# Two gelu buffers, sums of squares on VectorE behind the residual, and a side product moved forward in a two-block network

## The reference, cut to what matters

```python
h = rms_norm(x, g_mix_pre)
z = h @ w_in                                   # pool, recurrent, gelu and gate columns
xc = causal_dwconv(u_rx, conv_w, conv_b)       # 4 taps
r, i = sigmoid(xc @ w_gates + b_gates)         # 16 heads of 64, block diagonal
a = exp(-8 r softplus(-lambda)); mult = sqrt(1 - a^2)
h_t = a_t h_{t-1} + mult i xc                  # scan over the tokens
y_rnn = (h * gelu(u_rg)) @ w_rg_out
merged = sigmoid(g1) * y_pool + sigmoid(g2) * y_rnn
x = x + rms_norm(merged @ w_o, g_mix_post)
up = rms_norm(x, g_ffn_pre) @ w_up             # 2 x 3072
x = x + rms_norm((gelu(causal_dwconv(up[:, :3072])) * up[:, 3072:]) @ w_down, g_ffn_post)
gate = sigmoid(rms_norm(x, g_ple_gate) @ w_ple_gate)
x = x + gate * rms_norm(p @ w_ple_proj, g_ple_post)   # p: 1024 x 256
```

## Time and profile before

| | |
|---|---|
| median of 3 runs | 3355.74 us (3354.76 to 3365.66) |
| the profiled execution's own time | 3357.36 us |
| its span, first to last instruction | 3355.5 us |
| PE busy | 3221.1 us (96%) |
| PEld busy | 2582.4 us (77%) |
| DVE, ACT, POOL busy | 1538.5, 748.9, 1122.4 us |
| mean granted clock of PE | 0.994 of 2.4 GHz |
| mean transfer rate over the span | 62 GB/s |

### The profile page before, as it was taken

How to read it: one execution, slowest core, us unless ns; L and a number is a source line. 1 busy time by engine, 2 the same in 40 slices (tenths; PEclk the granted TensorE clock), 3 DMA queues, 4 the chain that set the end, 5 groups by cost and what they waited for, 6 DMA issues and landing times.

```text
span 3355.5 us, 41945 instructions
## 1 busy us (share of the span) xinstructions
PE 3221.1 (96%) x17662; PEld 2582.4 (77%) x17662; DVE 1538.5 (46%) x1625; ACT 748.9 (22%) x961; POOL 1122.4 (33%) x525
## 2 busy tenths in 40 slices
PE   6999998999889999899999999999999999999999
PEld 5877876787668788798576788788788888888757
DVE  3134428328822423824766601442553154255476
ACT  1011225112211122511334501112301011001241
POOL 2232220135532232044133344453144344434323
PEclk9999999999999999999999999999999999999999
DMA  6210111332131011112111111112211111111212
GB/s 235 70 32 14 39 35 48 126 137 84 61 119 38 14 38 47 57 42 109 63 51 38 38 44 54 38 54 97 76 49 45 50 50 44 50 50 45 81 44 75
DMA packets 59243, 208.16 MB, mean 62 GB/s; under 512 B 5856, under 2 KB 7648, under 8 KB 59104
## 3 DMA queue, kind: packets, MB, share of 16 engines
q1 hardware_dynamic: 42240, 143.15, 13.3%
q10 hardware_dynamic: 16864, 62.97, 5.0%
HBM read 188.27 MB, written 17.83 MB: 61 GB/s over the span
## 4 chain that ended last, share of the span: by engine, by line
PE 75%; DVE 16%; ACT 5%; DMA 2%; issue 1%; ACTq 0%; DVEq 0%
PE ps L541 65%; DVE Sb L1748 3%; PE ps L800 2%; DMA modfirst<-modw 1%; DVE stage L1839 1%; PE ps L523 1%; PE ps L568 1%; PE ps L710 1%; PE ps L1037 1%; PE ps L625 1%; DVE xc L1970 1%; DVE Y L1834 1%; DMA xin<-xT 1%; PE ps L947 1%; DVE stage L1854 1%
## 5 line engine op out<-in xcount | busy, mean ns | idle before, releaser
L467 POOL TENSOR_TENSOR w_hi<-raw,pool_zero 128x1024 fp32r<-128x1024 f32 (+2 forms) x242 | 454.0, 1876 | 2139.1 <-PE ps L541 2065.7
L469 POOL TENSOR_TENSOR w_lo<-raw,w_hi 128x1024 fp32r<-128x1024 f32 (+2 forms) x242 | 633.4, 2617 | 19.0
L541 PE MATMUL ps<-h_hi,w_hi 128*128 128x512 f32 (+1 forms) x1832 | 491.0, 364 | 26.5 <-ACT QK L1101 15.4
L541 PE MATMUL ps<-g_hi,w_hi 128*128 128x512 f32 x1568 | 490.5, 394 | 10.2 <-DVE g_lo L1574 5.2
L541 PE MATMUL ps<-g_lo,w_hi 128*128 128x512 f32 x1568 | 483.1, 389 | 0.0
L541 PE MATMUL ps<-g_hi,w_lo 128*128 128x512 f32 x1568 | 482.8, 389 | 0.0
L541 PE MATMUL ps<-h_lo,w_hi 128*128 128x512 f32 (+1 forms) x1832 | 469.7, 352 | 0.0
L541 PE MATMUL ps<-h_hi,w_lo 128*128 128x512 f32 (+1 forms) x1832 | 469.4, 352 | 0.0
L541 PEld LDWEIGHTS ps<-h_hi,w_hi 128*128 128x128 f32 x1832 | 301.0, 189 | 100.2 <-issue 23.3
L541 PEld LDWEIGHTS ps<-g_hi,w_hi 128*128 128x128 f32 x1568 | 292.9, 188 | 82.6 <-issue 9.4
L541 PEld LDWEIGHTS ps<-g_lo,w_hi 128*128 128x128 f32 x1568 | 294.4, 188 | 61.5
(11 more groups left out here) (312 smaller groups left out, 3451.2 us busy)
## 6 DMA issues: line engine op xcount, KB each, us to landing
raw<-s SPq DMA_DIRECT2D x226, 512.0 KB, 3.5
modring<-modw ACTq DMA_DIRECT2D x32, 512.0 KB, 4.7
xin<-xT ACTq DMA_DIRECT2D x1, 5120.0 KB, 18.2
x_saved<-Y ACTq DMA_DIRECT2D x1, 5120.0 KB, 16.3
xin<-x_saved ACTq DMA_DIRECT2D x1, 5120.0 KB, 17.6
modfirst<-modw SPq DMA_DIRECT2D x4, 1024.0 KB, 10.8
modfirst<-modw ACTq DMA_DIRECT2D x4, 1024.0 KB, 19.4
x_saved<-Y ACTq DMA_DIRECT2D x1, 4096.0 KB, 11.7
```

Source lines behind the costliest of these rows:

```text
L467: G.tensor_tensor(w_hi[s][:, :n], raw[s][:, :n], zero.to_broadcast([P, n]), ALU.add).then_inc(hi_done, 1)
L469: G.tensor_tensor(w_lo[s][:, :n], raw[s][:, :n], w_hi[s][:, :n].bitcast(F32), ALU.subtract)\
L541: last = T.matmul(ps[:, o + c0:o + c0 + size], wt[s][:, kk], xx[:, k, t0:t0 + size], start=(x == 0 and n == 0), stop=(x == k_n - 1 and n = ...
```

## The change

- *Recurrent stage:* the gelu goes alternately to two buffers (`gelus`); ACT evacuates it first in a chunk, then takes the previous high part; `xb` of the next chunk is evacuated behind tanh, ahead of the square root. The gate products stand behind step k = 4.
- *FFN:* the one-column products of the squares of each tile leave `first_pair`; DVE adds the squares after the last low part, and PE sums the total once inside slab 2, behind step 3, and spreads the inverse behind step 6. The waits of `first_pair` for evacuation and for split stand apart.
- *The end:* x and `p` are read in before the last eight FFN slabs and `p` is split among them. Two slabs of the side product stand ahead of the column sum, the third ahead of the spread, the others behind it; the fillers go. Full-row roots and reciprocals give way to those of 8 columns. The residual, high and low parts and `first_pair` go as in the FFN. The gate slabs are scaled by DVE into three buffers (`gates`), ACT applies sigmoid in place, and the normalisation of the side product is summed and spread in slab 3; the eight scalings of the side product, then three gatings, come ahead of the gate input 3 on DVE.

The core of the diff:

```diff
     def rnn_gate_maps(c):
         def maps(k):
-            if k != 3:
+            if k != 4:
                 return
             pe.wait_ge(tab_in, 112)
             pe.wait_ge(rnn_xc, c + 1)
...
-    def token_means(sq, first, last):
+    def token_means(m, total):
+        pe.wait_ge(sq_added, m)
         for t in range(SEQ // P):
-            ins = T.matmul(ps[:, 4 * BANK + t:4 * BANK + t + 1], sq[:, t * P:(t + 1) * P], ones[:, 0:1],
-                           start=(first and t == 0), stop=last, skip_group_check=True)
-        ins.then_inc(stat_used, 1)
+            last = T.matmul(ps[:, 4 * BANK + t:4 * BANK + t + 1], total[:, t * P:(t + 1) * P], ones[:, 0:1],
+                            start=True, stop=True, skip_group_check=True)
+        last.then_inc(stat_used, 1)
...
-        for s in range(2):
-            pe.wait_ge(split_done, g + s + 1)
-            pe.wait_ge(evac_done, g + s - 1)
-        keep_busy(0, 9)
+        pe.wait_ge(evac_done, g)
+        keep_busy(0, idle)
+        pe.wait_ge(split_done, g + 1)
         for x in range(KD + lag):
             if x < KD:
                 pe.wait_ge(sp_lo, SPLITS[name] + x + 1)
                 part(0, x)
-            if 1 <= x <= KD:
-                pe.wait_ge(stat_sq, squared + x)
-                token_means(C2[:, 7 + x, :], x == 1, x == KD)
+            if x == lag:
+                pe.wait_ge(split_done, g + 2)
             if x >= lag:
                 part(1, x - lag)
...
+    def ffn_scale(k):
+        if k == 3:
+            token_means(2, C2[:, 8, :])
+        if k == 6:
+            spread_inverse(2, 4)
     for f in range(FF_GROUPS):
         gf = G_FFN + 24 * f
         if f == 0:
             slab(gf + 2, 0, g_hi, g_lo, KD, SEC, 2, first=True, bank=6,
-                 between=lambda k: spread_inverse(2, 4) if k == 0 else None)
+                 between=ffn_scale)
...
-    keep_busy(6, 8)
-    sumsq_added(2, sq_g[:, 0, :])
-    keep_busy(6, 18)
-    sumsq(34)
-    for n in range(8):
-        keep_busy(6, {0: 13, 2: 22}.get(n, 0))
-        slab(G_PLEP + n, n % 2, p_hi, p_lo, 2, SEC, 2, SPLITS["p"] if n == 0 else None)
-    gemm(G_PLEG, 2, g_hi, g_lo, SEC, 2, SPLITS["h4"])
-    sumsq_added(3, C2[:, 8, :])
-    with pe.Fori(1, 4) as j:
+    for n in range(2):
+        slab(G_PLEP + n, n, p_hi, p_lo, 2, SEC, 2, SPLITS["p"] if n == 0 else None)
+    token_means(3, sq_g[:, 0, :])
+    for n in range(2, KD):
+        slab(G_PLEP + n, n % 2, p_hi, p_lo, 2, SEC, 2)
+        if n == 2:
+            spread_inverse(3, 6)
+    first_pair(G_PLEG, g_hi, g_lo, "h4", 5)
+    def gate_scale(k):
+        if k == 3:
+            token_means(4, C2[:, 8, :])
+        if k == 6:
+            spread_inverse(4, 4)
+    def ple_scale(k):
+        if k == 4:
+            token_means(5, fft[:])
+        if k == 7:
+            spread_inverse(5, 4)
+    slab(G_PLEG + 2, 0, g_hi, g_lo, KD, SEC, 2, first=True, bank=6, between=gate_scale)
+    slab(G_PLEG + 3, 1, g_hi, g_lo, KD, SEC, 2, between=ple_scale)
+    with pe.Fori(2, 4) as j:
         for s in range(2):
             slab(j * 2 + (G_PLEG + s), s, g_hi, g_lo, KD, SEC, 2)
+gates = [T2[:, 0, :], ffc[:], fft[:]]
...
+    evac(G_RNN, xb[:, 3:], SEQ, 2)
     for c in range(8):
-        if c:
-            act.wait_ge(rnn_xc, c)
-        evac(G_RNN + 2 * c, xb[:, 3:], SEQ, 2)
+        evac(G_RNN + 2 * c + 1, gelus[c % 2], SEQ, 2, ACT.Gelu_apprx_tanh)
         if c:
             rnn_high(c - 1)
-        evac(G_RNN + 2 * c + 1, B2[:, 1, :], SEQ, 2, ACT.Gelu_apprx_tanh)
         act.wait_ge(rnn_gates, c + 1)
         own.link(A.activation(B2[:, 2, :], ps[:, 4 * BANK:6 * BANK], ACT.Sigmoid, bias=vcol("b_gates", c)))
         A.activation(B2[:, 3, :], ps[:, 6 * BANK:8 * BANK], ACT.Sigmoid, bias=vcol("b_gates", 8 + c))\
             .then_inc(rnn_act, 1)
         A.activation(B2[:, 4, :], B2[:, 2, :], ACT.Exp, scale=lru_c[:, 0, c:c + 1])
         A.activation(B2[:, 5, :], B2[:, 2, :], ACT.Tanh, scale=lru_c[:, 1, c:c + 1]).then_inc(rnn_m2, 1)
+        if c < 7:
+            act.wait_ge(rnn_xc, c + 1)
+            evac(G_RNN + 2 * c + 2, xb[:, 3:], SEQ, 2)
         act.wait_ge(rnn_mult, 2 * c + 1)
         A.activation(B2[:, 7, :], B2[:, 6, :], ACT.Sqrt).then_inc(rnn_mult, 1)
...
+        if f == FF_GROUPS - 1:
+            act.wait_ge(slab_done, gf + 16)
+            act.dma_start(p_raw[:], pT.rearrange("k p t -> p k t")).then_inc(tab_in, 16)
+            act.dma_start(x_kept[:], x_saved.rearrange("k p t -> p k t")[:, :, CTX:]).then_inc(xr_in, 16)
         for n in range(KD):
+            if f == FF_GROUPS - 1 and n == 2:
+                act.wait_ge(tab_in, 160)
+                highs("p", 2, lambda k: p_raw[:, k, :], lambda k: p_hi[:, k, :], lambda k: None)
...
-                    square(n - 1, B2[:, n - 1, :], sq_g)
+                    hidden_square(n - 1)
     act.wait_ge(acc_used, 8 * (FF_GROUPS - 1))
-    square(KD - 1, B2[:, KD - 1, :], sq_g)
-    act.dma_start(C2[:, 0:8, :], x_saved.rearrange("k p t -> p k t")[:, :, CTX:]).then_inc(xr_in, 16)
-    std(26, T2[:, 2, :])
-    squares(48, lambda k: B2[:, k, :], lambda k: act.wait_ge(xn_ready, 24 + k + 1))
-    act.dma_start(C2[:, 0:2, :], pT.rearrange("k p t -> p k t")).then_inc(tab_in, 16)
-    std(34, C2[:, 7, :])
-    act.wait_ge(tab_in, 160)
-    highs("p", 2, lambda k: C2[:, k, :], lambda k: p_hi[:, k, :], lambda k: None)
-    highs("h4", KD, lambda k: C2[:, 8 + k, :], lambda k: g_hi[:, k, :], tmp_ready("h4"))
-    for n in range(KD):
+    hidden_square(KD - 1)
+    def ple(n):
         evac(G_PLEP + n, C2[:, n, :], SEQ, 2)
-    act.wait_ge(sp_lo, SPLITS["h4"] + 8)
-    for n in range(KD):
-        act.wait_ge(evac_done, G_PLEP + n + 1)
+    ple(0)
+    ple(1)
+    roots(19)
+    ple(2)
+    behind = {0: (3, 4), 1: (5,), 2: (6, 7)}
+    for k in range(KD):
+        act.wait_ge(xn_ready, 24 + k + 1)
+        if k == 3:
+            act.wait_ge(slab_done, G_PLEP + KD)
+        A.activation(g_hi[:, k, :], B2[:, k, :], ACT.Copy, scale=vcol("g_ple_gate", k)).then_inc(sp_hi, 1)
+        square(k, B2[:, k, :])
+        for n in behind.get(k, ()):
+            ple(n)
+    A.activation(fft[:], C2[:, 0, :], ACT.Square).then_inc(stat_sq, 1)
+    act.wait_ge(sq_added, 4)
+    square(1, C2[:, 1, :])
+    square(2, C2[:, 2, :])
+    roots(20)
+    square(3, C2[:, 3, :])
+    square(4, C2[:, 4, :])
+    keep_scale(4)
+    for n in range(5, KD):
         square(n, C2[:, n, :])
     for n in range(KD):
         if n == 2:
-            std(35, T2[:, 2, :])
-        if n >= 2:
-            act.wait_ge(out_ready, n - 1)
-        evac(G_PLEG + n, T2[:, n % 2, :], SEQ, 2, ACT.Sigmoid)
+            roots(21)
+        act.wait_ge(evac_done, G_PLEG + n + 1)
+        A.activation(gates[n % 3], gates[n % 3], ACT.Sigmoid).then_inc(gate_ready, 1)
...
+    def add_square(k, first, total=C2[:, 8, :], sq=None):
         dve.wait_ge(stat_sq, first + k + 1)
-        ins = V.tensor_tensor(sq[:, 0, :], sq[:, 0, :], sq[:, k, :], ALU.add)
+        ins = V.tensor_tensor(total, total, C2[:, 8 + k, :] if sq is None else sq, ALU.add)
...
+    for k in range(1, KD):
+        add_square(k, 24)
...
-    rsqrt(5, rs)
+                    add_square(n - 1, 32, sq_g[:, 0, :], sq_g[:, hidden_square_at(n - 1), :])
+                if f == FF_GROUPS - 1 and n == 4:
...
+    add_square(KD - 1, 32, sq_g[:, 0, :], sq_g[:, hidden_square_at(KD - 1), :])
+    inverse_columns(5)
     dve.wait_ge(xr_in, 64)
-    for k in range(KD):
-        own.link(V.scalar_tensor_tensor(B2[:, k, :], B2[:, k, :], vcol("g_ffn_post", k), rs, ALU.mult, ALU.mult))
-        V.tensor_tensor(B2[:, k, :], B2[:, k, :], C2[:, k, :], ALU.add).then_inc(xn_ready, 1)
-    rs2 = C2[:, 7, :]
-    rsqrt(6, rs2)
-    lows("p", 2, lambda k: C2[:, k, :], lambda k: p_hi[:, k, :], lambda k: p_lo[:, k, :])
-    lows("h4", KD, lambda k: C2[:, 8 + k, :], lambda k: g_hi[:, k, :], lambda k: g_lo[:, k, :],
-         lambda k: V.scalar_tensor_tensor(C2[:, 8 + k, :], B2[:, k, :], vcol("g_ple_gate", k), rs2,
-                                          ALU.mult, ALU.mult))
+    dve.wait_ge(rs_ready, 3)
+    for k in range(KD + 1):
+        if k < KD:
+            own.link(V.scalar_tensor_tensor(B2[:, k, :], B2[:, k, :], vcol("g_ffn_post", k),
+                                            ps[:, 6 * BANK:8 * BANK], ALU.mult, ALU.mult))
+            V.tensor_tensor(B2[:, k, :], B2[:, k, :], x_kept[:, k, :], ALU.add).then_inc(xn_ready, 1)
+        if k:
+            dve.wait_ge(sp_hi, SPLITS["h4"] + k)
+            V.scalar_tensor_tensor(g_lo[:, k - 1, :], B2[:, k - 1, :], vcol("g_ple_gate", k - 1),
+                                   g_hi[:, k - 1, :].bitcast(F32), ALU.mult, ALU.subtract).then_inc(sp_lo, 1)
     for k in range(1, KD):
-        add_square(k, 48)
-    rsqrt(7, rs)
+        add_square(k, 40)
+    for k in range(1, 3):
+        add_square(k, 48, fft[:])
+    inverse_columns(6)
+    dve.wait_ge(scale_ready, 2)
+    def gate_input(n):
```

(35 more changed lines are left out.)

52 lines of the change are left out of this document (25 added, 27 removed).

## The result

The changed kernel takes **3323.97 us** in the median of four runs (3320.58 to 3328.67); the kernel before, run beside it, 3356.03 (3354.76 to 3365.66). The ratio is 0.9895, with a 95% interval of 0.9873 to 0.9918: 32 us, or 1.0%, less. The profiled execution took 3320.58 us, with a span of 3318.8, where the sum in the prediction came to 3319.4.

A forecast was written before the change was run, and what follows sets the result against it. PE was taken to bound the kernel, busy 96% of the span, with waits hidden in that share. Terms -20 + 6 - 24 = -38 us from 3357.36 gave 3319.4, forecast 3318 us as median; own range 3308 to 3328, 8-in-10 range 3304 to 3336.

The forecast's parts named there:

- The bound and the recurrent stage: Recurrent stage: ACT and DVE loop falls to about 25.0 us, PE bounds at 25.28; -20 us, bounds -22 and 0.
- The first rival: Recurrent stage: both splits fall on DVE, a turn takes about 27.4 us, gain 5 instead of 20; 3333 us, chance 0.15.
- The FFN boundary: Between output product and FFN: PE work saved is given back through additions, splits and waiting; +6 us, bounds 0 and +9.
- the gap: FFN, before slab 3: PE idles 12 us instead of 1.3, restarting at about 2426.
- the clock: FFN, after PE's idling before slab 3: 1.7 us added for a lower clock.
- The end: After the last FFN slab: copy of x hidden, fillers gone, DVE sets the pace; -24 us, bounds -38 and -16.
- The delay by POOL: Last part: splits of three small and two large slabs delay DVE by 6.8 us, between 0 and 12.
- the reading in which PSUM inputs are held too: Last part: the eight scalings would take one more split, 4.3 us more at the end.
- the remark on the cover: Last part: the early request hides the copy of x; without that cover its 12.6 us would return.
- POOL hardly touching DVE: Rival, last part: splits barely delay DVE, the end gives -36 and the FFN boundary +3; 3303 us, chance 0.15.
- the copy not hidden: Rival, last part: copy of x competes with weight loads, loads or POOL fall behind by 12.6 us; 3331, chance 0.05.
- the clock did go down: Rival, whole kernel slower: clock stays at 1.2 GHz after PE idles; 100 us there gives 3368 us; chance 0.03.

The follow-up runs named there:

- second profile of the changed kernel: The changed kernel run again with nothing edited, on another chip beside the kernel before: 3323.82 us, ratio 0.9887.
- the two halves: The changed kernel with the gelu buffers alone (xb evacuated behind the square root), 3332.23 us; with the early xb alone (one gelu buffer), 3340.50 us.
- the second chip: Kernel before 3361.04 us; with only the recurrent change 3338.15; with the FFN boundary change too 3347.56; changed kernel with that boundary put back 3313.05.

## Why the prediction was right

*The bound and the recurrent stage* (-20 forecast, -21.7 by the table, of which 0.9 is no gain of the change: the 16 products of the spread ahead of the residual took 2.05 us instead of 2.96, and take 2.83 in the second profile of the changed kernel). The loop of 28.34 lost 2.35 and 0.96 us in the two halves, and PE became the bound with 25.2 us, 0.1 under the 25.28 of the working. The convolution ended 22.0 us after the gate products, as forecast, and DVE waits between chunks, so the splits of POOL that fall on it (operations of 3.3 us) are absorbed. The first rival, a loop that stays with DVE, would have shown 27 us; the loop set the pace only where one half was left out (25.99 and 27.38). That the two were close was read rightly: the loop alone would be 25.03, within 0.2 us of PE's 25.2.

*The FFN boundary* (+6 forecast, +8.6 by the table, +9.4 by the medians of the second chip; the bound was +9). The pair ended earlier and the work saved on PE was given back as idle time (7 x 1.84 is 12.9 us, not 12.5; no term of the sum hangs on it). Two estimates were met closely: the total came 16.1 us after the last low part, where 16.5 was worked out, and the gap is 12.21 where 12 was said. **The term that was too small is the clock.** The prediction took 1.7 us from the earlier trace rows, a pause of 2.7 us; after 12.2 us of idling seven pairs took 6.1 us instead of 3.2, and the whole FFN came out 2.8 us longer. That is 1.1 us of the miss. It also took the column sum and three steps at full pace, 5.9 us, where they took 7.60: 1.7 more, which the second profile of the kernel doesn't have. The two make up the 2.6 us by which the term missed (8.6 for 6), all but 0.2. The path that the prediction followed (additions, sum, three steps, spread, chain) does set when slab 3 starts; but the additions on it are no reason for the length of the gap, which stayed with one addition for seven.

*The end* (-24 forecast, -24.8 by the table, -25.1 by the medians). The delay by POOL was taken at 6.8 us: from the first residual operation to the last low part it is 36.3 us (3172.9 to 3209.2) instead of 29.4, so 6.9. The eight scalings, which have one input in SBUF and one in PSUM, took 10.50 us, 1.31 each, although POOL made a `w_lo` in that time (3253.5 to 3255.9, 2.41 us, as long as alone). The GPSIMD Engine Reference of the Trainium skill, section Key points, names contention only for DVE instructions in a two-port mode or with two SBUF inputs. The trace agrees; the reading in which PSUM inputs are held too would have added up to 4.3. The wait for the gate input 3 came out at 11.9 for 12.4, the tail from the last product to the end of the span at 7.9 for 8.0. Only the remark on the cover was wrong: without the early copy of x the residual starts 5.5 us later, not 12.6, because the chain of the column sum would hide the rest.

*The rivals.* POOL hardly touching DVE (3303) fell with the 6.9 us; the copy not hidden fell with the chain; the clock did go down, to 0.68 and 0.76 in the means of two short stretches, and came back some 6 us after PE had restarted in the one and 4 us in the other. How near the sum came to its profiled execution (1.2 us) is luck in good part: the terms missed by -1.7, +2.6 and -0.8 us and nearly cancel, and the runs of the same kernel lie up to 8 us apart.

*What stays open:* what decides, from run to run, whether the clock falls behind the same short wait; why the change gave 32 us on one chip and 38.9 on another; and what an earlier spread would give.

## What to carry to other kernels

Work taken from the busiest engine is worth nothing where the chain that frees its buffers doesn't get shorter: seven of eight column sums went, and the kernel is some 9 us faster with that boundary as it was. Before moving a sum, follow what waits for its result and in which order the engine that must release the next bank gets there; one instruction behind fourteen others that nothing on TensorE waited for cost 12 us, and moving it forward gave 16 with the clock. Price a cover by what else is late when it goes, not by the length of the transfer.
